# In each slot of the attention, the transposes go between the two halves of the score pieces

## The chip, the cores and the metric

The kernel runs on one core of one Trainium2 chip. The metric is device time in microseconds (us), the median of several executions. TensorE makes the matrix products, VectorE (DVE in rows), ScalarE (ACT) and GpSimd (POOL) do the rest, and SyncE (SP) issues most transfers.

## The reference

A decoder layer on x of shape (1, 2048, 1024): RMS norm, differential attention, residual, RMS norm, a mixture of 32 experts, residual, final RMS norm. The change touches the attention alone:

```python
for each of 8 heads, for each block of 128 queries:
    s = einsum('iqd,ikd->iqk', q, k) * scale + bias    # i = 0, 1: two score maps of one head
    s = where(rel >= 0, s, -inf)                       # causal
    p = softmax(s, axis=-1)
    a = p[0] - lam * p[1]
    o = a @ v                                          # v: 128 wide
```

## The kernel before

`build` calls `project` (norm, queries, keys and values), `attend` (the attention), `mix_and_route`, `run_experts` and `finish`, one after the other. Only `attend` is changed.

**Rows, pieces, units.** A row r is one block of 128 queries of one head: 8 heads of 16 rows. Four rows make a quad. The quads of a head come in the order 2, 0, 3, 1, so their rows hold 9 to 12, 1 to 4, 13 to 16 and 5 to 8 blocks of 128 keys. A row's scores, for each of its two maps m, are one piece of up to 1024 keys or, if the row is longer, a rest and then a piece of 1024: 384 pieces in all. A unit is a quad and a block of 128 keys: 40 to a head, 320 in all.

**TensorE** does three things, called S, T and V here, with a fourth once a quad:
- S, `score(c)` (L638 to L656): piece c, two matmuls for each 512 keys, into the half c % 2 of `ps_s`. It first waits until VectorE has taken piece c - 2 from that half.
- T, `turn(u)` (L667 to L675): up to four 128x128 transposes of the mixed probabilities of unit u, into one of two halves of `ps_t`. The first T of a quad waits for `mixed`, that is until GpSimd has mixed the quad's four rows.
- V, `add_v(u)` (L677 to L690): the product of unit u's transposed block and v, added up in `ps_o`. It waits until ScalarE has copied T's result out (`aT`).
- U, `turn_back(g)`, the quad's result transposed, once a quad.

**Slots.** The order is written out at build time. Slot n, for n from -18 to 327, holds the pieces `slots[n]`, then T of unit n, then V of unit n - 2. The pieces are dealt to slots so that their cost runs ahead of the transposes by a fixed lead. Of the 320 slots that have a T, 50 hold no piece, 185 one and 85 two. One slot of two is slot 1; the other 84 are twelve places that come again every 40 slots, in seven periods (h = 0 to 6): slots 20, 21, 22, 23, 26, 29, 30, 31, 33, 34, 36 and 41, plus 40h. Their pieces have, in keys: 128+1024 (slots 20, 21), 256+1024 (22, 23), 384+1024 (26), 512+1024 (29), 128+128 (30), 256+256 (31), 384+512 (33), 512+640 (34), 640+1024 (36), 768+1024 (41). The last head's transposes (slots 280 and on) share slots with the rest of the scores until slot 298 and have none of these places.

**VectorE** follows the same slots: for each piece `take(c)` (L583 scales the far part and finds its maximum, L586 adds the bias to the last 256 keys), after a row's last piece `peaks(r)` (L599), then `weigh(r)` (L607, L612) for rows whose exponentials were placed one slot before. L612 makes the row's coefficient `coef`. **ScalarE** in slot n copies T's result (L537) and then does the exponentials placed there (L548). **GpSimd** takes the rows in order: it waits for `coef` of the row (L612), scales map 1 by it (L516) and adds it to map 0 (L518), which sets `mixed`.

Of the kernel before, what the change touches and what calls it, by code (L numbers as in the profile page):

```python
# [318 lines left out]
def attend(nc, io, keep, scratch, sem):  # L319
# [24 lines left out]
    def tiles(u):  # L344
        g, k = units[u]
        return 4 - max(0, k - 4 * quads[g][1])

    BEGIN, END = -LEAD // 4, NU + 8
    slots, c, scored_cost, turned_cost = {}, 0, 0.0, 4 * BEGIN
# [9 lines left out]
    def ring(capacity):  # L359

        at, live, offsets, frees, freed = 0, [], [], [], -1
        for r, (g, i) in enumerate(rows):
            w = (i + 1) * P
            if at + w > capacity:
                at = 0
            while any(o < at + w and at < o + n for _, o, n in live):
                freed = live.pop(0)[0]
            live.append((r, at, w))
            offsets.append(at)
            frees.append(freed)  # L370
            at += w
        return offsets, frees
# [26 lines left out]
    with ExitStack() as ctx:  # L399
# [38 lines left out]
        def p0(r, k0, k1):  # L438
            return p0_ring[:, p0_at[r] + k0:p0_at[r] + k1]
# [196 lines left out]
        @block.tensor  # L636
        def _(pe):
            def score(c):  # L638
                r, m, k0, n = pieces[c]
                g, i = rows[r]  # L640
                h = quads[g][0]
                if c == first_piece[r]:
                    if r % 16 == 0:
                        pe.wait_ge(k_in[h % 2], 48 * (h // 2 + 1))
                    if r % 4 == 0:
                        pe.wait_ge(q_in[g % 2], 64 * (g // 2 + 1))
                if c >= 2:

                    pe.wait_ge(taken, c - 1)
                a = i % 4  # L650
                for j in range(0, n, 512):
                    e = min(512, n - j)
                    for hl in (1, 0):
                        mm = pe.matmul(ps_s[:, c % 2, j:j + e], q_st[:, g % 2, hl, m, a * P:(a + 1) * P],  # L654
                                       k_st[h % 2][:, m, k0 + j:k0 + j + e], start=hl == 1, stop=hl == 0)
                mm.then_inc(scored, 1)  # L656

            def ps_t_free(t):

                if t >= 2:  # L660
                    kind, x = turns[t - 2]
                    if kind == "T":
                        pe.wait_ge(t_out, x + 1)
                    else:
                        pe.wait_ge(o_set, x + 1)

            def turn(u):  # L667
                g, k = units[u]
                t = turn_of["T", u]
                if u == first_unit[g]:  # L670
                    pe.wait_ge(mixed, 4 * g + 4)
                ps_t_free(t)
                for a in range(4 - tiles(u), 4):
                    mm = pe.transpose(ps_t[:, t % 2, a * P:(a + 1) * P], p0(4 * g + a, k * P, (k + 1) * P), ident[:, :])  # L674
                mm.then_inc(turned, 1)  # L675

            def add_v(u):  # L677
                g, k = units[u]
                h = quads[g][0]
                a0 = 4 - tiles(u)  # L680
                pe.wait_ge(t_out, u + 1)
                if u == first_unit[g]:
                    if g % 4 == 0:
                        pe.wait_ge(v_in[h % 2], 16 * (h // 2 + 1))
                    if g >= 2:

                        pe.wait_ge(oT_set, g - 1)
                last = u == last_unit[g]
                pe.matmul(ps_o[:, g % 2, a0 * P:], v_st[:, h % 2, k, :], aT[:, u % A_RING, a0 * P:],  # L689
                          start=k == 0, stop=last).then_inc(summed, 1)  # L690

            def turn_back(g):
                t = turn_of["U", g]
                pe.wait_ge(oT_set, g + 1)
                ps_t_free(t)
                for a in range(4):
                    mm = pe.transpose(ps_t[:, t % 2, a * P:(a + 1) * P], oT[:, a * P:(a + 1) * P], ident[:, :])
                mm.then_inc(turned, 1)

            for n in range(BEGIN, END):  # L700
                for c in slots[n]:
                    score(c)
                if 0 <= n < NU:
                    turn(n)
                if 0 <= n - V_LAG < NU:
                    add_v(n - V_LAG)
                for g in range(NG):
                    if last_unit[g] + V_LAG + 2 == n:
                        turn_back(g)
# [915 lines left out]
```

## Time and profile before

| | |
|---|---|
| three executions | 2624.05, 2628.01, 2629.54 us |
| median | 2628.01 us |
| the profiled execution | 2633.91 us, of it 2632.3 us span |
| mean granted TensorE clock | 0.936 |
| the attention's TensorE work | from 612 us to about 1357 us of the span |
| one period of 40 slots (one head) | 88.4 us |

Times in rows are from the start of the span. A row of the timeline gives start, duration, engine, line, instruction, output and inputs, shape and count; consecutive instructions of one engine and line are merged into one row under the shape of the first. In brackets stands the idle time ahead of it and who ended it. Matmuls are pipelined: a duration reaches beyond the start of the next one, so that steps are read from start to start. A first score matmul that follows V is listed just after V's second half has started, and so carries some 0.40 us of V's work.

### The profile page before, as it was taken

The page shows a single profiled execution, that of the slowest core. Times are in us where ns is not written, and L with a number is a line of the kernel's source. Part 1 is how long each engine was busy: PE and PEld are TensorE (multiplying, and loading weights), DVE is VectorE, ACT ScalarE, POOL GpSimd, SP SyncE. Part 2 cuts the span into 40 slices and gives each one's busy share as a digit, 9 for nine tenths or more (in the row PEclk, how much of TensorE's full clock was granted, in tenths as well). Part 3 has the DMA queues.
Part 4 walks back from the last instruction along what each step waited for, and adds up shares of the span by engine and source line. Part 5 has one row for each costly group of instructions (what it writes and reads, how often), then busy time and mean ns, then how long its engine had stood idle before and what let it go on. Part 6 is the DMA issues. An engine that isn't in the chain of part 4 may idle for free. (4 is left out here: it accounts for less than half of the span.)

```text
span 2632.3 us, 36772 instructions
## 1 busy us (share of the span) xinstructions
PE 2350.6 (89%) x11480; PEld 1881.4 (71%) x11480; DVE 1380.5 (52%) x2803; ACT 1217.5 (46%) x1642; POOL 728.5 (28%) x558
## 2 busy tenths in 40 slices
PE   4999999996999999999958999488999999999981
PEld 3888889994666666666637878366788888788760
DVE  6212121104667666766634666657655655666663
ACT  5011111112666666666652544346554554655553
POOL 0000000002676666675620011222222222222220
PEclk7999999996999999999979889689999999999995
DMA  5333334216324443442143433279888788888867
GB/s 184 130 115 130 112 127 116 63 46 158 74 77 111 108 97 77 110 96 75 41 128 121 172 110 112 103 254 362 291 303 289 230 272 279 276 295 305 303 185 271
DMA packets 207628, 441.45 MB, mean 168 GB/s; under 512 B 19081, under 2 KB 56113, under 8 KB 205490
## 3 DMA queue, kind: packets, MB, share of 16 engines
q1 hardware_dynamic: 187186, 375.27, 42.5%
q0 software_dynamic: 19008, 60.91, 9.3%
q10 hardware_dynamic: 1344, 4.19, 0.6%
q8 instruction: 42, 0.69, 0.1%
q14 instruction: 48, 0.39, 0.1%
HBM read 338.55 MB, written 101.76 MB: 167 GB/s over the span
## 5 line engine op out<-in xcount | busy, mean ns | idle before, releaser
L583 DVE TENSOR_SCALAR_CACHE_REDUCE p_ring<-ps_s 128x256 f32<-128x256 f32 (+7 forms) x352 | 277.8, 793 | 160.3 <-PE ps_s L654 154.1
L1373 DVE TENSOR_TENSOR gu_lo<-gu_raw,gu_hi 128x2048 fp32r<-128x2048 f32 x128 | 293.3, 2291 | 129.3 <-issue 78.7
L518 POOL TENSOR_TENSOR p_ring<-p_ring 128x1152 f32<-128x1152 f32 (+15 forms) x128 | 321.6, 2512 | 10.7
L548 ACT ACTIVATE p_ring<-p_ring,shift 128x1152 f32<-128x1152 f32 (+15 forms) x256 | 305.9, 1197 | 18.2 <-DVE shift L599 18.2
L689 PE MATMUL ps_o<-aT,v_st 128*128 128x512 f32 (+3 forms) x640 | 292.8, 541 | 0.0
L537 ACT ACTIVATE aT<-ps_t 128x512 f32<-128x512 f32 (+1 forms) x320 | 168.1, 531 | 230.2 <-PE ps_t L674 230.1
L1315 ACT ACTIVATE gu_hi<-gu_raw 128x2048 fp32r (+1 forms) x128 | 237.9, 1915 | 30.1 <-PEq L740 15.5
L654 PE MATMUL ps_s<-k,q_st 128*128 128x512 f32 (+3 forms) x640 | 210.8, 458 | 35.1 <-DVE top L586 20.5
L1447 PE MATMUL ps_g<-gu_hi,xT_lo 128*128 128x512 f32 x720 | 235.3, 408 | 7.5 <-DVE xT_lo L1388 7.5
L1447 PE MATMUL ps_g<-gu_lo,xT_hi 128*128 128x512 f32 x720 | 227.6, 397 | 0.0
L1447 PE MATMUL ps_g<-gu_hi,xT_hi 128*128 128x512 f32 x720 | 227.4, 397 | 0.0
L516 POOL TENSOR_SCALAR p_ring<-p_ring,coef 128x1152 f32<-128x1152 f32 (+15 forms) x128 | 150.5, 1175 | 252.2 <-DVE coef L612 249.4
L654 PE MATMUL ps_s<-k_st,q_st 128*128 128x512 f32 (+3 forms) x640 | 204.9, 444 | 12.5 <-DVE top L586 12.0
L674 PE MATMUL ps_t<-ident,p_ring 128*128 128x128 f32 x1088 | 179.4, 282 | 25.9 <-POOL p_ring L518 25.9
L654 PEld LDWEIGHTS ps_s<-k,q_st 128*128 128x128 f32 x640 | 125.5, 210 | 102.9 <-issue 38.4
L1381 DVE TENSOR_TENSOR d_lo<-d_raw,d_hi 128x2048 fp32r<-128x2048 f32 x64 | 146.7, 2293 | 84.0 <-ACT d_hi L1322 49.8
L674 PEld LDWEIGHTS ps_t<-ident,p_ring 128*128 128x128 f32 x1088 | 138.6, 144 | 69.7 <-POOL p_ring L518 27.8
L238 DVE TENSOR_TENSOR stage<-ps,stage 128x512 fp32r<-128x512 f32 x64 | 44.3, 692 | 274.6 <-ACT stage L185 274.6
L185 ACT ACTIVATE stage<-ps 128x512 fp32r<-128x512 f32 x64 | 38.3, 598 | 314.6 <-PE ps L301 314.6
L1280 POOL DMA_INDIRECT x_rows<-y_sb,lists x45 | 98.5, 2190 | 286.3 <-ACT y_sb L1333 274.5
L654 PEld LDWEIGHTS ps_s<-k_st,q_st 128*128 128x128 f32 x640 | 117.7, 196 | 79.3 <-issue 43.9
L1343 ACT ACTIVATE act_g<-ps_g 128x512 f32<-128x512 f32 x45 | 27.0, 600 | 292.3 <-PE ps_g L1447 292.3
(215 smaller groups left out, 4316.8 us busy)
## 6 DMA issues: line engine op xcount, KB each, us to landing
gu_raw<-in_moe_w_gate SPq DMA_DIRECT2D x128, 512.0 KB, 9.9
gu_raw<-in_moe_w_up SPq DMA_DIRECT2D x128, 512.0 KB, 11.5
d_raw<-in_moe_w_down SPq DMA_DIRECT2D x64, 1024.0 KB
qk<-stage SPq DMA_DIRECT2D x64, 512.0 KB, 2.8
q_st<-qk SPq DMA_DIRECT2D x128, 256.0 KB, 5.1
w_raw<-in_diff_w_in POOLq DMA_DIRECT2D x12, 1024.0 KB, 6.7
k<-qk SPq DMA_DIRECT2D x8, 1024.0 KB, 12.3
v<-stage SPq DMA_DIRECT2D x64, 128.0 KB, 1.8
```

The costliest lines, as they stand in the source:

```text
L516: pool.tensor_scalar(p1(r, 0, w), p1(r, 0, w), coef[:, r % 8, :], 0.0, ALU.mult, ALU.add).then_inc(scaled, 1)
L518: pool.tensor_tensor(p0(r, 0, w), p0(r, 0, w), p1(r, 0, w), ALU.add).then_inc(mixed, 1)
L537: nc.scalar.activation(aT[:, n % A_RING, a0 * P:], ps_t[:, turn_of["T", n] % 2, a0 * P:], ACT.Copy).then_inc(t_out, 1)
L548: nc.scalar.activation(p, p, ACT.Exp, bias=shift[:, r % 8, m:m + 1], accum_out=sums[:, r % 8, m:m + 1]).then_inc(raised, 1)
L583: ins = nc.vector.tensor_scalar(p(r, k0, k0 + far), ps_s[:, c % 2, 0:far], SCALE, None, ALU.mult, ALU.max, accum_out=top[:, r % 4, m, col: ...
L654: mm = pe.matmul(ps_s[:, c % 2, j:j + e], q_st[:, g % 2, hl, m, a * P:(a + 1) * P], k_st[h % 2][:, m, k0 + j:k0 + j + e], start=hl == 1, s ...
L674: mm = pe.transpose(ps_t[:, t % 2, a * P:(a + 1) * P], p0(4 * g + a, k * P, (k + 1) * P), ident[:, :])
L689: pe.matmul(ps_o[:, g % 2, a0 * P:], v_st[:, h % 2, k, :], aT[:, u % A_RING, a0 * P:], start=k == 0, stop=last).then_inc(summed, 1)
L1315: nc.scalar.activation(gu_hi[:, j * GC:(j + 1) * GC], raw(half, j), ACT.Copy).then_inc(gu_hi_set, 1)
L1373: nc.vector.tensor_tensor(gu_lo[:, j * GC:(j + 1) * GC], raw(half, j), gu_hi[:, j * GC:(j + 1) * GC].bitcast(F32), ALU.subtract).then_inc( ...
L1381: nc.vector.tensor_tensor(d_lo[:, j * DC:(j + 1) * DC, :], d_raw[:, j], d_hi[:, j * DC:(j + 1) * DC, :].bitcast(F32), ALU.subtract).then_i ...
L1447: mm = pe.matmul(ps_g[:, half, :], x[:, cs], w[:, c, half, :], start=c == 0 and k == 0, stop=c == KC - 1 and k == 2)
```

## The change

In `tensor` of `attend`, a slot's pieces are cut in half. The first half, rounded up, is made, then T, then the other half, then V. Where a slot holds no piece or one, the order is as before; where it holds two, it was S, S, T, V and is now S, T, S, V. The other engines' programs are not changed, and no instruction is added or removed.

```diff
             for n in range(BEGIN, END):
-                for c in slots[n]:
+                ahead = slots[n][:(len(slots[n]) + 1) // 2]
+                for c in ahead:
                     score(c)
                 if 0 <= n < NU:
                     turn(n)
+                for c in slots[n][len(ahead):]:
+                    score(c)
                 if 0 <= n - V_LAG < NU:
                     add_v(n - V_LAG)
```

## Rows read from the trace of the kernel before

**Rows 1.** What TensorE waited for, 612 to 1365 us: total, times, longest.

```profile
PE ps_s L654 <- DVE top L586: 32.5, 31, 4.9
PE ps_t L674 <- POOL p_ring L518: 25.9, 8, 3.3
```

**Rows 2.** Timeline of TensorE and VectorE, period 0, from T of slot 20.

```profile
705.55 0.60 PE L674 MATMUL ps_t<-ident,p_ring 128*128 128x128 f32 x4
...
705.91 0.95 DVE L583 TENSOR_SCALAR_CACHE_REDUCE p_ring<-ps_s 128x768 f32<-128x768 f32 x1
...
706.45 2.03 PE L654 MATMUL ps_s<-k_st,q_st 128*128 128x128 f32 x6
...
708.31 0.60 PE L674 MATMUL ps_t<-ident,p_ring 128*128 128x128 f32 x4
...
708.51 0.96 DVE L583 TENSOR_SCALAR_CACHE_REDUCE p_ring<-ps_s 128x768 f32<-128x768 f32 x1 [0.99 <-PE ps_s L654]
...
708.75 1.02 PE L689 MATMUL ps_o<-aT,v_st 128*128 128x512 f32 x2
...
711.10 0.96 DVE L583 TENSOR_SCALAR_CACHE_REDUCE p_ring<-ps_s 128x768 f32<-128x768 f32 x1 [0.50 <-PE ps_s L654]
...
716.03 1.48 PE L654 MATMUL ps_s<-k_st,q_st 128*128 128x512 f32 x4
717.35 0.60 PE L674 MATMUL ps_t<-ident,p_ring 128*128 128x128 f32 x4
```

**Rows 3.** TensorE's timeline, V with no S behind it (slots 38, 39).

```profile
748.27 1.02 PE L689 MATMUL ps_o<-aT,v_st 128*128 128x512 f32 x2
749.13 0.27 PE L674 MATMUL ps_t<-ident,p_ring 128*128 128x128 f32 x1
```

**Rows 4.** Timeline, period 0, slots 29 to 33, VectorE, TensorE and GpSimd.

```profile
726.80 0.96 DVE L583 TENSOR_SCALAR_CACHE_REDUCE p_ring<-ps_s 128x768 f32<-128x768 f32 x1 [0.22 <-PE ps_s L654]
...
727.39 1.22 PE L654 MATMUL ps_s<-k_st,q_st 128*128 128x128 f32 x4
...
728.45 0.41 PE L674 MATMUL ps_t<-ident,p_ring 128*128 128x128 f32 x2
728.55 0.22 DVE L612 SCALAR_TENSOR_TENSOR coef<-sums,neg_lam,inv 128x1 f32<-128x1 f32 x1
...
730.40 3.21 POOL L518 TENSOR_TENSOR p_ring<-p_ring 128x1408 f32<-128x1408 f32 x1
...
732.85 0.78 DVE L612 SCALAR_TENSOR_TENSOR coef<-sums,neg_lam,inv 128x1 f32<-128x1 f32 x1
...
735.36 3.45 POOL L518 TENSOR_TENSOR p_ring<-p_ring 128x1536 f32<-128x1536 f32 x1
735.77 3.06 DVE L612 SCALAR_TENSOR_TENSOR coef<-sums,neg_lam,inv 128x1 f32<-128x1 f32 x1
```

**Rows 5.** TensorE's timeline, period 0, second piece of slot 34 to slot 35.

```profile
735.74 0.88 PE L654 MATMUL ps_s<-k_st,q_st 128*128 128x512 f32 x4 [0.76 <-DVE top L586]
736.45 0.62 PE L674 MATMUL ps_t<-ident,p_ring 128*128 128x128 f32 x4
736.91 1.02 PE L689 MATMUL ps_o<-aT,v_st 128*128 128x512 f32 x2
739.57 1.20 PE L654 MATMUL ps_s<-k_st,q_st 128*128 128x512 f32 x4 [1.64 <-DVE top L586]
```

**Rows 6.** The same place in period 3: GpSimd, VectorE, TensorE.

```profile
1000.42 3.44 POOL L518 TENSOR_TENSOR p_ring<-p_ring 128x1536 f32<-128x1536 f32 x1
...
1000.46 3.42 DVE L612 SCALAR_TENSOR_TENSOR coef<-sums,neg_lam,inv 128x1 f32<-128x1 f32 x1
...
1004.62 1.19 PE L654 MATMUL ps_s<-k,q_st 128*128 128x512 f32 x4 [2.01 <-DVE top L586]
```

**Rows 7.** Five engines' busy us, granted clock, DMA share, GB/s; slot 35, periods 0, 3.

```profile
739.50:744.50 5.00, 4.93 (x27) 3.88 (x28) 4.38 (x17) 2.00 (x5) 2.24 (x5) 1.00 0.48 110
...
1004.60:1009.60 5.00, 4.98 (x18) 3.54 (x18) 2.92 (x10) 2.00 (x5) 1.49 (x3) 0.66 0.39 91
```

## The prediction

> **Where the time is.** I read the table of times first: the attention is some 745 of 2632 us, and it repeats itself every 88.4 us. Then the waits of TensorE over that stretch [rows 1]. The reader is to see that TensorE is the bound there and that two partners hold it up. VectorE, slow to empty the score buffer, costs 32.5 us in 31 waits. GpSimd, slow to mix a quad, costs 25.9 us in 8 waits, the first T of slot 16 of each head. The second kind sits in slots with no piece, which keep their order. Only the first kind can be touched. Last I read the timeline slot by slot, from start to start.
>
> **What the parts cost.** T then V: 708.31 to 708.75, so T is 0.44 for four transposes (0.11 each). V is 0.86 (748.27 to 749.13). A piece of 1024 keys behind V takes 1.32 to the next start (716.03 to 717.35), of which 0.40 is V's tail: 0.92, or 0.09 for each 100 keys, so 0.12 for 128 and 0.23 for 256 [rows 2, 3].
>
> **What the edit does.** No instruction comes or goes, no transfer is issued or moved: SP's and GpSimd's queues are as before. In the 84 slots of the seven periods T steps ahead of the second piece. (Slot 1 holds such a pair too; TensorE is still filling its first buffers there, and I count nothing.) So the second piece starts up to 0.44 later, and T ends earlier by that piece. What waits for T, ScalarE's copy, is not late now: VectorE and GpSimd end the waits [rows 1]. What waits for the second piece is VectorE's take, with the row's maxima and the coefficient L612 queued behind it.
>
> **Slots 20 to 23: the waits stay.** At face value T fills a wait here. Slot 21 takes 1.86 from S to T (706.45 to 708.31) and needs 0.40 + 0.12 + 0.92 = 1.44, so 0.42 is lost ahead of the 1024 piece. But look at what sets it. Small and big pieces alternate between the two halves of `ps_s`, so every big piece uses the same half: it can start only when the big piece of the slot before is taken. VectorE starts those takes at 708.51 and 711.10, 2.59 apart, while TensorE's work for such a slot is 0.23 + 0.92 + 0.44 + 0.86 = 2.45. The 0.14 between is TensorE's loss in slots 22 and 23 [rows 2, 3]. The loop S, take, next S in that half has the same length with T on either side of the big piece. Order within the slot can't shorten it.
>
> What remains is how the chain is entered and left. It is entered at slot 20's big piece, now 0.44 later. VectorE starts that take 0.36 after T's start (705.55, 705.91), where 0.20 is usual (708.31, 708.51): 0.16 of it was its own lateness and is absorbed. So the chain runs 0.44 - 0.16 = 0.28 late. It is left at slot 23, where T no longer follows the big piece: 0.28 - 0.44 = -0.16, a gain of 0.16. Slots 24 to 28 have no wait to lose (slot 25 is the one measured at 0.92 above).
>
> **Slots 29 to 35: the gain is handed to a chain that does not go through TensorE.** In slot 29 T has three transposes, 0.33, and goes ahead of the 1024 piece, which so starts at -0.16 + 0.33 = +0.17. Its take begins at 726.80, and VectorE makes the coefficient of a finished row only behind it, at 728.55. From there [rows 4]: GpSimd scales and adds (L518 from 730.40, 3.21 long, ends 733.61). The next coefficient, L612 at 732.85, lasts 0.78 where 728.55 took 0.22: it ends as that L518 ends. GpSimd then starts the next row's L518 at 735.36, ends 738.81, and L612 of 735.77 lasts 3.06, to 738.83. Only then does VectorE take the first piece of slot 34, and TensorE, idle for 1.64, starts slot 35 at 739.57 [rows 4, 5]. So slot 35's start follows the take of slot 29's big piece by a chain of VectorE and GpSimd, and comes 0.17 later. That T now fills 0.44 of the 0.76 wait in slot 34 (735.74) brings nothing: slot 35 waits for something else, and what TensorE saves it adds to the idle time there. In period 3 the same pair ends as late (L518 1000.42, L612 1000.46) [rows 6].
>
> The same holds inside: slot 30's second piece waits for slot 29's take, so T of slot 30 only fills time that slot 29 moved. After slot 35 nothing waits for VectorE until slot 41, and slots 36 and 41 come out even. The sum: +0.17 for a period, x 7 = **+1.2 us**. If VectorE's 0.16 were not absorbed it would be +0.33, +2.3 us. If the chain kept its old time and only the 0.16 of slot 23 counted, -1.1 us.
>
> **Joints.** T then S, and S then V, are new. T then V is 0.44 behind long matmuls and 0.46 in slot 34 (736.45 to 736.91) [rows 2, 5]. So a joint may cost 0 to 0.02; below nothing too, as S then S goes away. 84 x 2 x 0.02 = 3.4 us up, half that down. Both are hidden where a wait follows; I take 0.
>
> **The clock.** This is where the change does cost. Ahead of slot 35 TensorE idles 1.64 us in period 0 (1.65, 1.66 in the next two) and the granted clock stays at 1.00, 2.4 GHz; in period 3 it idles 2.01 (2.01, 2.01, 1.99 to the last), and the mean granted clock of the 5 us behind is 0.66, that is 0.34 x 2 x 5 = 3.4 us at 1.2 GHz [rows 5 to 7]. Half of that is lost, at most 1.7 us; I take 1.5. After the change 0.44 of work moves from behind slot 34's second piece to ahead of it, into the earlier wait, so the last idle grows by 0.44: 1.64 becomes 2.08 in periods 0 to 2, beyond the 2.01 that dropped the clock, and 2.01 becomes 2.45 in the others. Three new drops would be 4.5 us. Since the idle is one of several close by, not each need fall; I take two, **+3.0 us**, ends 0 and 4.5.
>
> **Sum.** +1.2 + 3.0 = +4.2 us, 0.16%. Against the profiled execution's own 2633.9 (span 2632.3) that is 2638.1; that execution lies 5.9 us, 0.22%, above the median, so against the median 2628.0 it is **2632 us**. A difference within 0.2%, 5.3 us, is about what a measurement of this kernel can't tell from no change. So: no measurable change, leaning to slower. Its own range: 0 to +7 with the joints, and the median's scatter of some 2 us: 2626 to 2637.
>
> **Rivals.**
> - *T fills the waits, as slot order suggests.* Then slot 21's 0.42, 0.14 each in slots 22 and 23, 0.24 at slot 30 (two transposes; 727.39 to 728.45 is 1.06 where 0.40 + 0.12 + 0.12 is needed), and 0.44 at slot 34 are saved: 1.38 a period, 9.7 us in seven, 2618 us. For it: each of these waits stands right ahead of a second piece. Against it: the 2.59 loop and the chain of slots 29 to 35, which T does not enter. Chance 0.12.
> - *VectorE gets in ahead of GpSimd.* In slot 34 of periods 3 to 6 L612 starts 0.04 after L518 and so waits 3.4 us [rows 6]. Were it 0.05 earlier against GpSimd it would take 0.22. Then slot 35 starts about its whole idle time, 2.0 us, earlier and keeps its clock (1.5): 3.5 x 4 = 14 us less, 2614 us. Against it: both start from the same event, the end of the L518 before, so a shift of TensorE moves them together. The Trainium skill (SBUF — State Buffer, section Who interferes with whom) says that a VectorE instruction with two SBUF inputs and a GpSimd one that reads SBUF exclude each other for a whole instruction, and the one issued first wins; the two L612 that end with an L518 agree, by 0.02 us. Chance 0.04.
> - *Slower: the clock falls in every period, and for longer.* With 2.08 and 2.45 us of idle, the three new drops come (4.5), and in periods 3 to 6 the longer idle makes the stretch at 1.2 GHz half as long again (0.75 x 4 = 3.0); with 1.2 that is +8.7, 2637 us. It decides from the third drop on: 1.2 + 4.5 = 5.7 is already beyond 0.2%. For it: rows 7's 0.66 after 2.01 us. Against: 1.66 left the clock alone, and where the edge between lies no row shows. Chance 0.24.
> - The edit does what it says wherever a slot has two pieces; that those are too few to matter (85 of 320) is part of the forecast, chance 0.60.
>
> **Chances and range.** Faster: 0.12 + 0.04, less 0.02 for cases in which they are half true and the clock takes it back: 0.14. Slower: the slower rival's 0.24, and 0.04 of the forecast, its upper end with dear joints: 0.28. Same 0.58. The range takes in the fills from 2618 and the clock case with joints up to 2640: 2619 to 2639 leaves out some 0.15.
>
> **What would show it.** In the profile after: TensorE's wait for VectorE in sum is no smaller (within 3 us), with more of it ahead of slot 35, 2.0 to 2.5 us each; big takes of slots 21 to 23 still 2.59 apart; L612 still ends with L518 in slots 33 and 34; granted clock 0.66 behind slot 35 in period 0 as well. The period is 88.5 to 90 us. Wrong if the 2.59 shrinks, if slot 35 starts earlier against slot 16 of its head, or if L612 of slot 34 takes 0.22.

## The result and the profile after

The changed kernel takes 2639.23 us, median of 8 executions (2633.12 to 2642.29), against 2627.72 (2624.05 to 2629.96) for the kernel before in as many: ratio 1.0041, 95% interval 1.0031 to 1.0052. It is slower by 0.4%, some 11 us. The forecast of 2632 us was too low by 7 us, and "no measurable change" did not hold: the difference is twice the 5.3 us under which the prediction put it, and slower was the outcome it gave a chance of 0.28. The end of its range was just reached: 2639 us is 1.0042 times its 2628.01, against the measured 1.0041; as a time, 2639.23 lies 0.2 us above.

What TensorE waited for in the attention, after (total, times, longest); before it was [rows 1]:

```profile
PE ps_s L654 <- DVE top L586: 34.1, 27, 5.0
PE ps_t L674 <- POOL p_ring L518: 26.0, 8, 3.3
```

Four waits fewer and 1.6 us more: of the waits ahead of slot 34's second piece those of periods 3 to 6 (0.39 each) went and the others shrank; the waits ahead of slot 34's first piece (0.60 to 0.81) and the long ones ahead of slot 35 grew. TensorE in period 0 after, slot 21, start by start, and in a second view VectorE's takes of the big pieces of slots 20, 21 and 22:

```profile
706.48 0.74 PE L654 MATMUL ps_s<-k_st,q_st 128*128 128x128 f32 x2
707.05 0.62 PE L674 MATMUL ps_t<-ident,p_ring 128*128 128x128 f32 x4
707.59 1.19 PE L654 MATMUL ps_s<-k_st,q_st 128*128 128x512 f32 x4
708.62 1.02 PE L689 MATMUL ps_o<-aT,v_st 128*128 128x512 f32 x2
```

```profile
706.22 0.96 DVE L583 TENSOR_SCALAR_CACHE_REDUCE p_ring<-ps_s 128x768 f32<-128x768 f32 x1 [0.17 <-PE ps_s L654]
708.82 0.96 DVE L583 TENSOR_SCALAR_CACHE_REDUCE p_ring<-ps_s 128x768 f32<-128x768 f32 x1 [1.07 <-PE ps_s L654]
711.41 0.96 DVE L583 TENSOR_SCALAR_CACHE_REDUCE p_ring<-ps_s 128x768 f32<-128x768 f32 x1 [0.60 <-PE ps_s L654]
```

The order is S, T, S, V now, and the takes stand 2.60 and 2.59 apart, as before (705.91, 708.51, 711.10 [rows 2]). The chain of slots 29 to 35 in period 0: first VectorE, then GpSimd, then TensorE.

```profile
728.75 0.22 DVE L612 SCALAR_TENSOR_TENSOR coef<-sums,neg_lam,inv 128x1 f32<-128x1 f32 x1
...
732.30 1.53 DVE L612 SCALAR_TENSOR_TENSOR coef<-sums,neg_lam,inv 128x1 f32<-128x1 f32 x1
...
735.97 3.05 DVE L612 SCALAR_TENSOR_TENSOR coef<-sums,neg_lam,inv 128x1 f32<-128x1 f32 x1
```

```profile
730.60 3.21 POOL L518 TENSOR_TENSOR p_ring<-p_ring 128x1408 f32<-128x1408 f32 x1
...
735.56 3.44 POOL L518 TENSOR_TENSOR p_ring<-p_ring 128x1536 f32<-128x1536 f32 x1
```

```profile
735.93 0.87 PE L654 MATMUL ps_s<-k_st,q_st 128*128 128x512 f32 x4 [0.33 <-DVE top L586]
736.65 1.07 PE L689 MATMUL ps_o<-aT,v_st 128*128 128x512 f32 x2
739.76 1.19 PE L654 MATMUL ps_s<-k_st,q_st 128*128 128x512 f32 x4 [2.04 <-DVE top L586]
740.78 0.60 PE L674 MATMUL ps_t<-ident,p_ring 128*128 128x128 f32 x4
741.22 1.86 PE L689 MATMUL ps_o<-aT,v_st 128*128 128x512 f32 x2
```

Against [rows 4, 5] each step is 0.20 later (728.55 to 728.75, 730.40 to 730.60, 735.36 to 735.56, 739.57 to 739.76). Slot 20, the first that the order touches, starts 0.06 later in this trace (704.32 before, 704.38 after), so 0.14 of the 0.20 belongs to the order. The second piece of slot 34 waits 0.43 less (0.76 to 0.33), the first of slot 35 waits 0.40 more (1.64 to 2.04). And V, 1.02 long before, lasts 1.86. The granted clock is the third figure from the end of these rows. The first two are of the trace after, behind slot 35 of period 0 (before: [rows 7]) and around slot 16 of head 2; the last is that slot 16 before:

```profile
739.59:744.59 5.00, 4.83 (x17) 3.29 (x18) 3.24 (x13) 2.00 (x5) 1.65 (x3) 0.67 0.41 104
872.50:882.50 10.00, 6.83 (x26) 5.79 (x27) 4.70 (x13) 3.67 (x8) 8.14 (x5) 0.66 0.09 27
```

```profile
869.16:879.16 10.00, 7.00 (x30) 5.68 (x31) 5.28 (x16) 4.66 (x9) 7.98 (x5) 0.83 0.09 27
```

In period 0 the clock that stayed at 1.00 in [rows 7] falls to 0.67 over five microseconds. In all seven periods after, that window reads 0.66 or 0.67; before, four of seven did. The second place is one that the prediction left out: around the first T of slot 16, which waits 3.3 us for GpSimd in every head, 0.83 over ten microseconds means 3.4 us at 1.2 GHz, and 0.66 means 6.8.

### The profile page after: what moved, and what is told of

The parts are those of the page before. It is cut to its first block and busy times, and to the rows that moved or that the text cites. A ratio compares the mean times of both kernels' runs of the same rounds, so it can differ in the third digit from the quotient of the medians.

```text
span 2637.5 us, 36772 instructions
## 1 busy us (share of the span) xinstructions
PE 2354.1 (89%) x11480; PEld 1885.8 (71%) x11480; DVE 1387.0 (53%) x2803; ACT 1218.6 (46%) x1642; POOL 727.0 (28%) x558
## 5 line engine op out<-in xcount | busy, mean ns | idle before, releaser
L518 POOL TENSOR_TENSOR p_ring<-p_ring 128x1152 f32<-128x1152 f32 (+15 forms) x128 | 321.6, 2513 | 10.7
L654 PE MATMUL ps_s<-k,q_st 128*128 128x512 f32 (+3 forms) x640 | 217.4, 463 | 35.7 <-DVE top L586 21.3
L654 PE MATMUL ps_s<-k_st,q_st 128*128 128x512 f32 (+3 forms) x640 | 211.6, 447 | 13.3 <-DVE top L586 12.8
```

Source lines behind the costliest of these rows:

```text
L518: pool.tensor_tensor(p0(r, 0, w), p0(r, 0, w), p1(r, 0, w), ALU.add).then_inc(mixed, 1)
```

## The experiments

**Which slot carries the loss.** Slot 34 alone in the old order, then alone in the new one. The kernel before, on the same chip: 2629.27 us (23 executions).

```diff
-                ahead = slots[n][:(len(slots[n]) + 1) // 2]
+                ahead = slots[n] if n % 40 == 34 else slots[n][:(len(slots[n]) + 1) // 2]    # e1_not34
+                ahead = slots[n] if n % 40 != 34 else slots[n][:(len(slots[n]) + 1) // 2]    # e2_only34
```

> The changed kernel, but slot 34 of each period keeps the old order (S, S, T, V); the other eleven places are changed. Theory A (the clock): T ahead of slot 34's second piece lengthens the idle ahead of slot 35 by 0.44 us, and behind that idle TensorE runs at 1.2 GHz for 3.4 us, about 1.5 us lost in each of seven periods; the unprofiled executions of the kernel before mostly lack these drops. Then this kernel is back at 2627 to 2631 us, ratio to before 1.000 to 1.001. Theory B (the second pieces, 0.17 us late a period by the VectorE and GpSimd chain, and dearer joints T, S and S, V): most of the loss stays, 2635 to 2638 us, ratio 1.003 to 1.004.

> The kernel before, with only slot 34 of each period changed to S, T, S, V (seven slots in all). Theory A (the clock): nearly the whole loss, 2636 to 2639 us, ratio 1.003 to 1.004, and the idle ahead of slot 35 is 2.0 us or more in every period. Theory B (late second pieces, joints): seven slots of 84, no difference, 2627 to 2629 us.

e1_not34: 2633.56 us, ratio 1.0014 (1.0003 to 1.0024). e2_only34: 2637.97 us, 1.0032 (1.0022 to 1.0042). Seven slots bring 8.7 us, all the others 4.3: theory B, for which the first number should be the large one, falls. But e1 is above what theory A gave it, so something else is in the eleven other places.

**Second traces of both kernels.**

> The kernel before once more, for a second trace. Theory A: the granted clock falls behind slot 35 in fewer periods than the four of seven in the first trace (0 to 2), and the time is that much lower, 2625 to 2630 us. Theory B: four again, since it holds that the clock is alike in both kernels.

> The changed kernel once more, for a second trace. Theory A: the clock falls behind slot 35 in six or seven of seven periods, 2636 to 2642 us. Theory B: in about as many as in the kernel before.

2629.20 and 2639.45 us. The changed kernel again had the lower clock behind slot 35 in seven of seven periods, as theory A expected. The kernel before again had it in four, periods 3 to 6, not in 0 to 2: there theory A, as I put it, was wrong. The difference must then come from more than three new drops, and the count of the other place shows it. The table counts stretches of the lower clock in windows like those above (around slot 16 they start some 3 us ahead of T), in each trace, over the seven periods from T of slot 16 in head 0 to T of slot 16 in head 7. A stretch is 3.4 us at 1.2 GHz; a window of ten microseconds at 0.83 is one, at 0.66 two.

| kernel | stretches behind slot 35 | around slot 16 | length of the seven periods | less 1.4 us a stretch |
|---|---|---|---|---|
| before | 4 | 8 | 625.3 us | 608.5 |
| before again (e3) | 4 | 7 | 623.8 | 608.4 |
| after | 7 | 9 | 631.9 | 609.5 |
| after again (e4) | 7 | 11 | 634.2 | 609.0 |
| e1_not34 | 5 | 9 | 629.3 | 609.7 |
| e2_only34 | 6 | 10 | 630.8 | 608.4 |
| e5_after_fill | 0 | 6 | 617.5 | 609.1 |
| e6_before_fill | 0 | 6 | 616.9 | 608.5 |

Eight lengths that differ by 17 us fall within 1.3 us once each stretch is counted at 1.4 us. The 1.4 is fitted to them: it lies below the 1.7 that half of 3.4 us would be. What is left between after and before is 0.8 us (609.25 and 608.45, means of two).

The row of e1 needs a reservation. Its trace holds three more stretches, one in each of periods 0 to 2, that began in slot 34, ahead of slot 35. Here is slot 34's second piece and V in period 2:

```profile
909.79 0.88 PE L654 MATMUL ps_s<-k_st,q_st 128*128 128x512 f32 x4 [0.75 <-DVE top L586]
911.17 1.92 PE L689 MATMUL ps_o<-aT,v_st 128*128 128x512 f32 x2
```

V lasts 1.92 in place of 1.02, but its end falls into what was the wait: slot 35 waits 0.56 there (0.41 in period 1, still less in period 0), where it waited 1.66 in the kernel before. These three are left out of the count because most of their cost lay in that wait; counted in, e1 has 17 stretches, and its last column would read 605.5, outside the 1.3 us. So e1's remaining loss goes with the lower clock as far as the 14 stretches behind slot 35 and around slot 16 show it, against 11 and 12 before; why its other places bring them is not shown.

Each row is one execution. That of e1 took 2637.92 us, 4.4 above its median, and that of e2 2630.43, 7.5 below its own, though e2's seven periods are the longer ones. The span outside the seven periods ranges from 1998 us (e2) to 2007 (e1, before), so the table explains the seven periods and not a median to a few microseconds.

**Keep the clock up by filling the idle time.** Both kernels, with matmuls whose result nobody reads in front of slot 35. (A matmul on f32 is two in the rows: six read x12.) The rows of e5, TensorE in period 0, and its clock windows in periods 0 and 3:

```diff
                 if 0 <= n - V_LAG < NU:
                     add_v(n - V_LAG)
+                if n % 40 == 34 and 0 < n < 300:
+                    ps_t_free(turn_of["T", n + 1])
+                    for _ in range(6):
+                        pe.matmul(ps_t[:, turn_of["T", n + 1] % 2, 0:P], ident[:, :], ident[:, :], start=True, stop=True)
```

> The changed kernel with six extra matmuls, identity times identity (128 columns each), behind V of slot 34 in each period, written to the half of the transposes' buffer that slot 35 overwrites: work without a result, some 1.3 us at full clock, laid into the idle time ahead of slot 35. Theory A (the clock is the cost): the clock stays up behind slot 35, 5 to 7 drops of 1.65 us go, 2625 to 2631 us, and the kernel equals the kernel before with the same filling within 3 us. Theory B (late pieces and joints): 2638 to 2640 us, 9 us or more above the kernel before with the filling.

> The kernel before with the same filling. Theory A: its drops in periods 3 to 6 go as well, 2621 to 2626 us. Theory B: no drop matters, 2628 to 2630 us.

```profile
735.80 1.50 PE L713 MATMUL ps_t<-ident 128*128 128x128 f32 x12
738.03 1.20 PE L654 MATMUL ps_s<-k_st,q_st 128*128 128x512 f32 x4 [0.72 <-DVE top L586]
739.06 0.60 PE L674 MATMUL ps_t<-ident,p_ring 128*128 128x128 f32 x4
739.50 1.02 PE L689 MATMUL ps_o<-aT,v_st 128*128 128x512 f32 x2
```

```profile
738.20:743.20 5.00, 5.00 (x27) 3.80 (x28) 4.28 (x15) 2.60 (x6) 2.25 (x5) 1.00 0.46 108
1003.53:1008.53 5.00, 5.00 (x27) 3.79 (x28) 4.29 (x15) 2.60 (x6) 2.25 (x5) 1.00 0.46 109
```

2620.98 us (12 executions) and 2620.96 us: ratios 0.9973 (0.9961 to 0.9985) and 0.9974 (0.9962 to 0.9985) to the kernel before on that chip, 2627.98. The 11 us between the two orders are gone: the medians differ by 0.02 us, the intervals leave some 3. V is 1.02 long again. This is the deciding pair: the change costs what the clock costs, and what else it costs is too small to measure here. The changed kernel even fell below the 2625 us that theory A gave it, the kernel before to the lower end of its 2621 to 2626; the table counts 6 stretches in each, against 16 and 18 after and 11 and 12 before. 42 matmuls without a result make both kernels faster than they were.

**Cut the chain instead.** L612 with one tensor operand and two scalars.

```diff
-                nc.vector.scalar_tensor_tensor(out=coef[:, r % 8, :], in0=sums[:, r % 8, 0:1], scalar=neg_lam[:, 0:1],
-                                               in1=inv[:, r % 16, 1:2], op0=ALU.mult, op1=ALU.mult).then_inc(coefed, 1)
+                nc.vector.tensor_scalar(coef[:, r % 8, :], sums[:, r % 8, 0:1], neg_lam[:, 0:1], inv[:, r % 16, 1:2],
+                                        ALU.mult, ALU.mult).then_inc(coefed, 1)
```

> The kernel before with L612 as a tensor_scalar: two scalar operands and one tensor operand in place of two tensor operands in SBUF. The theory of the chain (VectorE's L612 waits for GpSimd's L518, and slot 35 waits for both): L612 of slots 33 and 34 takes 0.2 us, the idle ahead of slot 35 shrinks from 1.9-2.5 to under 1 us, the clock stays up there, and 15 to 30 us go, 2600 to 2615 us. If the tensor_scalar waits for GpSimd just as well, nothing changes. Rival (slot 35 waits for something else): L612 short and the time within 3 us of before.

> The changed kernel with L612 as a tensor_scalar. With the long idle gone there is no clock to lose and nothing for the chain to hand on: theory A expects it within 3 us of the kernel before with the same L612. Theory B (late second pieces and joints cost by themselves): 5 to 10 us above it. If T then fills VectorE's waits as the order suggests, 5 to 10 us below it.

L612's 128 instances, after and in e8 (duration in ns: least, median, most):

```profile
L612 DVE SCALAR_TENSOR_TENSOR coef<-sums,neg_lam,inv x128: 218/220/3437, 631.8 to 1340.5; 128x1 f32<-128x1 f32 x128
```

```profile
L612 DVE TENSOR_SCALAR coef<-sums,neg_lam,inv x128: 272/273/277, 631.8 to 1297.3; 128x1 f32<-128x1 f32 x128
```

In the traces of e7 and e8 none of the 128 instances lasts longer than 277 ns, and the wait ahead of slot 35 is gone in every period. e7: 2604.76 us, ratio 0.9912 (0.9892 to 0.9931). e8: 2595.62 us, 0.9874 (0.9854 to 0.9893). With the short L612 the change is worth 9.1 us, the sign the slot order suggests: not the "within 3 us" that theory A gave, but the last alternative there.

**Where that gain sits.** Three kernels, all with the short L612: after (e9) and before (e10) with slot 16's idle time filled by eleven such matmuls at the end of slot 15, behind U, and nothing in slot 34; and after with slot 34 back in the old order and no filling (e11, the edit of e1).

> The changed kernel with the tensor_scalar L612, and eleven extra matmuls without a result (identity times identity, some 2.4 us) at the end of slot 15 of each head, ahead of the first T of slot 16, which waits 3.5 us for GpSimd. If the clock is what such an idle time costs there too, about one drop of 1.5 us for each of eight heads goes: 2582 to 2587 us against 2595.6 without the filling. If the clock falls for another reason, or the extra work delays T, 2595 us or more.

> The kernel before with the same L612 and the same filling in slot 15. The change's own worth with neither the chain nor the clock in play: the trace of the two kernels with the short L612 shows slot 34 cheaper by 0.4 to 0.7 us a period and slot 30 dearer by 0.14, slot 21 cheaper by 0.15: 3 to 5 us between this and the changed one, so 2587 to 2592 us. If the whole 9 us of the pair without filling was order, 2592 to 2596 us.

> The changed kernel with the tensor_scalar L612, but slot 34 in the old order. If the gain of the change under the short L612 is T filling the wait of slot 34's second piece, most of it is gone: 2601 to 2605 us, near the 2604.8 of the kernel before with that L612. If the other eleven places carry it, 2596 to 2598 us.

```diff
+                if n % 40 == 15 and 0 < n < NU:
+                    ps_t_free(turn_of["T", n + 1])
+                    for _ in range(11):
+                        pe.matmul(ps_t[:, turn_of["T", n + 1] % 2, 0:P], ident[:, :], ident[:, :], start=True, stop=True)
```

e9: 2589.42 us, the fastest (ratio 0.9851, 0.9830 to 0.9871). e10: 2592.14 us (0.9860, 0.9839 to 0.9881). e11: 2599.83 us (0.9894, 0.9873 to 0.9914). e9 missed its 2582 to 2587 us: the filling took 6.2 us (e8 to e9), less than the 1.5 for each of eight heads; e8's trace had 7 stretches to lose. TensorE in slots 34 and 35 of period 3, of e9 and then of e10:

```profile
978.35 0.60 PE L674 MATMUL ps_t<-ident,p_ring 128*128 128x128 f32 x4
978.91 0.88 PE L654 MATMUL ps_s<-k,q_st 128*128 128x512 f32 x4
979.62 1.07 PE L689 MATMUL ps_o<-aT,v_st 128*128 128x512 f32 x2
980.13 1.50 PE L654 MATMUL ps_s<-k,q_st 128*128 128x512 f32 x4
```

```profile
980.49 0.74 PE L654 MATMUL ps_s<-k,q_st 128*128 128x512 f32 x2
981.62 0.87 PE L654 MATMUL ps_s<-k,q_st 128*128 128x512 f32 x4 [0.39 <-DVE top L586]
982.33 0.62 PE L674 MATMUL ps_t<-ident,p_ring 128*128 128x128 f32 x4
982.79 1.02 PE L689 MATMUL ps_o<-aT,v_st 128*128 128x512 f32 x2
983.25 1.49 PE L654 MATMUL ps_s<-k,q_st 128*128 128x512 f32 x4
```

From V's start to slot 35's is 0.46 to 0.51 in both: nothing waits there. So the 0.39 that T now covers in slot 34 is time won. It was the same cover of 0.43 that won nothing in the changed kernel, where slot 35 waited for the chain. The seven periods take 584.2 us in e9's trace and 589.7 in e10's, neither with a stretch at 1.2 GHz: order alone is worth 5.5 us in these traces. The medians show 2.7 us, below the 3 to 5 expected; the two numbers don't agree, and order alone stays at 2.7 to 5.5 us. The rest of the 9.1 goes with the clock: the filling took 12.6 us from e7's kernel and 6.2 from e8's, and around slot 16 of the eight heads e7's trace has 10 stretches, e8's 7. e11 lost 4.2 of the 9.1 (3.2 if the 1.05 us between the two chips' runs of the kernel before is taken off): slot 34 holds a third to a half. 2599.83 lies between the two ranges expected; my "most of it" was too much.

## Why the prediction was right and wrong, by its steps

- **The waits stay in slots 20 to 23: right.** The takes stand 2.59 to 2.60 apart in both orders.
- **The gain is handed to a chain outside TensorE: right**, and its size nearly. +0.17 a period was forecast; period 0 shows 0.20, 0.14 of it from the order, and with the stretches taken out the seven periods differ by 0.8 us where +1.2 stood in the sum. e5 and e6, 0.02 us apart with some 3 us left open, say no more than that it is small. e7 and e8 show the chain was the reason: without it the same order wins.
- **L612 still ends with L518: right.** In slot 33 it came 0.55 earlier (732.85 to 732.30), as ScalarE's copy of T's result did (732.45 to 731.90), and waited 1.53 in place of 0.78 for the same event. The Trainium skill (SBUF — State Buffer, section Who interferes with whom) says that a VectorE instruction with at most one input from SBUF does not contend with GpSimd outside the two-port modes, and that one with two contends with a GpSimd instruction that reads SBUF. The traces of e7 and e8 agree: 277 ns at most where 3437 stood. The same section of the Trainium skill lets a tensor_scalar contend in those modes; none of the 256 of e7 and e8 did.
- **Joints at 0: right** as far as shown: the two filled kernels are 0.02 us apart (interval some 3 us), 168 joints included.
- **The idle grows beyond what drops the clock: right in kind, 1.64 to 2.04 in period 0 (2.08 forecast). This is the term that failed in size.** The sum took two of three new drops, +3.0 us, at most 4.5. All three came, at some 1.6 us in period 1 (from the start of slot 35 to V of slot 41 13.3 us before, 14.9 after). And the sum counted one place only. Slot 16's wait had been set aside because its slot has no piece and the wait is as long as before, 3.3 us at most. But the clock's answer to it was not constant: none, one stretch or two, 8 and 7 stretches before against 9 and 11 after. With these the two kernels are 11.5 and 17 stretches, 5.5 x 1.4 = 7.7 us, plus 0.8: 8.5 us, the difference of the seven periods in the traces (624.5 and 633.1; the 1.4 is fitted and the 0.8 is the rest, so the sum must come out). Why slot 16 has more of them after is open; two traces of each kernel are few for it, and no run changed that place alone without the short L612. The median difference is 11.5 us by 8 executions each; the 3 us between it and the four traces I can't place, and single traces scatter by more than that outside the seven periods. The period, 90.3 and 90.6 us on average (89.3 and 89.1 before), passed the 90 of the prediction for the same reason.
- **The base.** The forecast's sum was made on the profiled execution, 5.9 us above the median of the kernel before; the second trace was 2629.20. The profiled execution after lies at its median. The sum of seven periods alone doesn't carry that difference (625.3 and 623.8 in the two traces).
- The slower rival had the right sign and nearly the size (2637), by another way: the drops behind slot 35 were not longer in periods 3 to 6 (0.66 as before); there were more of them elsewhere.

## What to carry to other kernels

Before putting work into a wait, ask what the next long wait hangs on: if its end is set by other engines, the work moved only collects the idle time in one piece, and one piece of 2.0 us cost TensorE's clock (behind 32 of the 33 waits of 1.99 us and more ahead of slot 35 in the traces of both kernels, e1 and e2) where one of 1.65 did not (0 of 6). The length of one wait is no rule, though: in e1 the clock fell three times behind two waits of 0.8 us close together, and around slot 16 a wait of 3.3 us cost no, one or two stretches. Short waits spread out can be the cheaper arrangement. And count the clock in every place where it falls, also in those that the edit does not touch: their cost was not the same in two traces of one kernel.

## What the runs showed of the hardware that I had not expected

- Matmuls without a result pay: 42 of them behind slot 34 took 7 us off the kernel before and some 18 off the changed one (2639.23 to 2620.98, on another chip). With the short L612 and without those 42, 88 at the end of slot 15 took 6.2 (e8 to e9) and 12.6 (e7 to e10, each pair on two chips). In the filled places the granted clock stayed at 1.00.
- A scalar_tensor_tensor on 128x1 elements lasts 220 ns alone and up to 3437 beside GpSimd's tensor_tensor, until that ends; a tensor_scalar with two scalar operands for the same result lasted 272 to 277 in all 128 instances. The exchange took 23 us (0.9%) off the kernel before (e7).
- S between T and V costs TensorE nothing that the medians show: T ahead of S, S ahead of V, 168 new joints, and 0.02 us between e5 and e6, with some 3 us left open by the intervals.
